# Four input-projection panels as seven block products, with x kept in DRAM during token mixing

## What is computed

```python
u = rmsnorm(x, ng[1]) * (1.0 + sc2) + sh2
proj = u @ P['w_in'][l]                       # 1024 -> 2816 columns
p_conv, p_rwkv, p_pool, p_sb = jnp.split(proj, IN_SPLITS, axis=-1)
# A short gated conv, B RWKV-7, C causal pooling, D stick-breaking attention -> y_a .. y_d
for i, y_i in enumerate((y_a, y_b, y_c, y_d)):
    merged = merged + jax.nn.sigmoid(u @ P['w_gate'][l, i]) * (y_i @ P['w_branch'][l, i])
x = x + g2 * (merged @ P['w_out'][l])
```

## Time and profile before

| | before |
|---|---|
| median of 3 runs | 3027.72 us (3027.41 to 3027.86) |
| profiled execution | 3027.79 us |
| its span | 3026.1 us |
| PE busy | 2991.8 us (99%) |
| DVE busy | 1426.4 us (47%) |
| ACT busy | 411.8 us (14%) |
| POOL busy | 1472.0 us (49%) |
| chain that ended last | PE 92%, POOL 4%, DVE 3%, issue 1% |

### The profile page before, as it was taken

The page is one execution under the profiler, slowest core; times in us unless marked ns, Lnnn a source line. Parts: engine busy times, 40 slices in busy tenths (PEclk is TensorE's granted clock), DMA queues, the critical chain, the costliest instruction groups (busy, mean ns, idle before and its releaser), DMA issues.

```text
span 3026.1 us, 48463 instructions
## 1 busy us (share of the span) xinstructions
PE 2991.8 (99%) x19566; PEld 2460.4 (81%) x19566; DVE 1426.4 (47%) x3125; ACT 411.8 (14%) x782; POOL 1472.0 (49%) x1527
## 2 busy tenths in 40 slices
PE   8999999999999999999999999999999999999999
PEld 5889888677777878898878898876777778789987
DVE  4446522464444464565244564324444444555642
ACT  2000002212111120000010000032021111200000
POOL 4879530212220348895468894312212213599943
PEclk9999999999999999999999999999999999999999
DMA  6543223541111424322245322334411114222221
GB/s 256 201 189 117 98 100 130 172 140 42 54 57 58 144 90 158 109 84 91 88 163 230 127 84 87 136 115 151 129 59 54 54 70 151 70 84 84 84 87 68
DMA packets 73535, 337.81 MB, mean 112 GB/s; under 512 B 10592, under 2 KB 27744, under 8 KB 40288
## 3 DMA queue, kind: packets, MB, share of 16 engines
q1 hardware_dynamic: 63936, 312.03, 28.5%
q0 software_dynamic: 6816, 18.88, 2.1%
q10 hardware_dynamic: 2560, 3.80, 0.4%
HBM read 326.55 MB, written 6.02 MB: 110 GB/s over the span
## 4 chain that ended last, share of the span: by engine, by line
PE 92%; POOL 4%; DVE 3%; issue 1%; DMA 0%; ACT 0%; SPq 0%; POOLq 0%; DVEq 0%
PE ps L1003 91%; DVE ws L2295 1%; DVE u L2295 1%; POOL masked_room L901 0%; DVE y L2295 0%; DMA ws<-w_ada 0%; POOL ws L860 0%; POOL ws L863 0%; ACT ws L1974 0%; POOL ws L864 0%; POOL ring L914 0%; POOL ws L868 0%; POOL ws L866 0%; POOL ws L849 0%; PE ps L1793 0%
## 5 line engine op out<-in xcount | busy, mean ns | idle before, releaser
L2295 DVE TENSOR_TENSOR ws<-ws,ps 128x272 f32<-128x272 f32 (+4 forms) x1650 | 620.2, 400 | 1110.1 <-PE ps L1003 1085.7
L1003 PE MATMUL ps<-u,ring 128*128 128x272 f32 (+1 forms) x4448 | 1035.7, 383 | 6.2 <-ACT u L1974 1.7
L1003 PEld LDWEIGHTS ps<-u,ring 128*128 128x128 f32 x4448 | 799.3, 190 | 181.5 <-issue 21.4
L1003 PE MATMUL ps<-y,ws 128*128 128x272 f32 (+1 forms) x1616 | 343.3, 348 | 0.0
L1003 PEld LDWEIGHTS ps<-y,ws 128*128 128x128 f32 x1616 | 265.4, 190 | 36.5 <-issue 4.5
L1974 ACT ACTIVATE ws<-ws 128x272 f32<-128x272 f32 (+5 forms) x226 | 137.0, 623 | 1105.5 <-DVE ws L2295 1054.0
L1003 PE MATMUL ps<-y,ring 128*128 128x272 f32 (+1 forms) x1376 | 277.0, 341 | 2.8 <-POOL ws L868 2.8
L1003 PEld LDWEIGHTS ps<-y,ring 128*128 128x128 f32 x1376 | 219.0, 190 | 33.1 <-POOL ws L868 3.8
L846 POOL TENSOR_TENSOR masked_room<-ring 128x512 f32<-128x512 f32 (+1 forms) x36 | 46.8, 1299 | 401.9 <-PE ps L1003 170.7
L1974 ACT ACTIVATE ws<-ps 128x272 f32<-128x272 f32 (+1 forms) x270 | 102.7, 395 | 864.3 <-PE ps L1003 864.2
L1003 PE MATMUL ps<-proj,ring 128*128 128x272 f32 x832 | 200.3, 393 | 1.5 <-DVE proj L2295 1.5
(11 more groups left out here) (248 smaller groups left out, 3825.0 us busy)
## 6 DMA issues: line engine op xcount, KB each, us to landing
ring<-w_up SPq DMA_DIRECT2D x88, 1024.0 KB, 4.9
proj<-w_ada SPq DMA_DIRECT2D x45, 1024.0 KB, 7.6
ring<-w_down SPq DMA_DIRECT2D x32, 1024.0 KB, 4.8
ring<-w_gate SPq DMA_DIRECT2D x32, 1024.0 KB, 4.9
ws<-w_ada SPq DMA_DIRECT2D x26, 1024.0 KB, 5.0
ring<-w_in SPq DMA_DIRECT2D x22, 1024.0 KB, 4.9
ws<-cache SPq DMA_DIRECT2D x128, 128.0 KB, 3.2
ws<-cache POOLq DMA_DIRECT2D x128, 128.0 KB, 3.4
```

Of the source, the lines that this page charges most:

```text
L1003: return nc.tensor.matmul(out, lhsT, rhs, start=start, stop=stop, skip_group_check=skip)
L2295: return V.tensor_tensor(out, a, b, op)
```

## The change

Panels 7 to 10 of the input projection are made by seven products of four matmuls (`split_in`) in place of four halves of eight. POOL makes the weight sums for each panel, three ahead and one when a12 has been used, S3 and S4 in the panel's own room in the ring; S1 and S2 have new rooms `in_s1` and `in_s2` in `ws`, of which the first covers the end of attention's `sa`, so panel 7's first sum waits for attention's last product. POOL's cache loads for the last three rounds stand between the sums. ACT copies out two results per panel and DVE makes the other additions (`in_sum`) at places in pooling, convolution and between token shifts. The banks are 1, 2, 3 and 4, 5, 7 in turn; the transposition of `own1` goes to bank 6.

The token sums T1 to T4 are made once by POOL, early, right after u is complete (`mix_token_sums`), for these panels and for the gates. They lie in x's room (`mix_tok`): SP stores x to DRAM (`x_kept`) as soon as it is complete, and loads it back behind the last gate panel (gate 23); DVE waits for it before it adds the output projection. Semaphores, the helpers `in_blocks`, `in_products`, `in_weights`, `in_act`, `in_dve` (waits on counts) and `in_out` (the result's place in `proj`) and the changed `split_tok` are left out below, as are blank lines.

```diff
+IN_SPLIT = (7, 8, 9, 10)
+IN_BANKS = {7: (1, 2, 3), 8: (4, 5, 7), 9: (1, 2, 3), 10: (4, 5, 7)}
+IN_ACT = {"first": 1, "c11": 2}
+IN_DVE = {"U2": 1, "U3": 2, "c22": 3, "c21": 4}
...
-        newT, at1 = carve(at1, P)
+        newT = sa[:, 896:1024]
+        in_s1, at1 = carve(at1 - 256, 4, P)
+        in_s2, at1 = carve(at1, 4, P)
...
+        mix_tok = x[:, :, :].rearrange("p a (b n) -> p (a b) n", n=HALF).rearrange("p (s k) n -> p s k n", s=4)
...
+        in_first, in_second, in_third = last_inner[:, :], masked_room[:, 544:544 + HALF], rtail[:, 512:512 + HALF]
...
+                            sp_.dma_start(x_kept, x[:, :, :]).then_inc(x_saved.sem, 16)
...
+                        if stage == "gate" and i == 23:
+                            sp_.dma_start(x[:, :, :], x_kept).then_inc(x_back.sem, 16)
...
+                def mix_token_sums():
                     b11, b12, b21, b22 = u[:, 0:4, 0:HALF], u[:, 0:4, HALF:T], u[:, 4:8, 0:HALF], u[:, 4:8, HALF:T]
-                    pool.wait_ge(pool_pe.sem, pool_pe.upto(l, 1))
-                    nc.gpsimd.tensor_tensor(split_t12[:, 0], b12, b11, ALU.subtract).then_inc(sp_sums.sem, 1)
+                    pool.wait_ge(x_saved.sem, x_saved.upto(l, 1))
+                    pool.wait_ge(up_done.sem, up_done.upto(l, U0[1] + 16))
+                    pool.wait_ge(us_done.sem, us_done.upto(l, 2))
+                    nc.gpsimd.tensor_tensor(mix_tok[:, 0], b12, b11, ALU.subtract).then_inc(sp_sums.sem, 1)
                     pool.wait_ge(sp_sums.sem, sp_sums.upto(l, 1))
-                    nc.gpsimd.tensor_tensor(split_t12[:, 1], b22, split_t12[:, 0], ALU.subtract).then_inc(sp_sums.sem, 1)
+                    nc.gpsimd.tensor_tensor(mix_tok[:, 1], b22, mix_tok[:, 0], ALU.subtract).then_inc(sp_sums.sem, 1)
                     pool.wait_ge(sp_sums.sem, sp_sums.upto(l, 2))
-                    nc.gpsimd.tensor_tensor(split_t4a, b21[:, 0:3], split_t12[:, 1, 0:3], ALU.subtract).then_inc(sp_sums.sem, 1)
-                    nc.gpsimd.tensor_tensor(split_t4b, b21[:, 3], split_t12[:, 1, 3], ALU.subtract).then_inc(sp_sums.sem, 1)
-                    pool.wait_ge(rp_pe.sem, rp_pe.upto(l, 2))
-                    pool.wait_ge(rp_dve.sem, rp_dve.upto(l, 1))
-                    nc.gpsimd.tensor_tensor(split_t3, b22, b12, ALU.subtract).then_inc(sp_sums.sem, 1)
+                    nc.gpsimd.tensor_tensor(mix_tok[:, 3], b21, mix_tok[:, 1], ALU.subtract).then_inc(sp_sums.sem, 1)
+                    nc.gpsimd.tensor_tensor(mix_tok[:, 2], b22, b12, ALU.subtract).then_inc(sp_sums.sem, 1)
+                def in_weight_sums(j):
+                    panel_wait(pool, l, "in", j)
+                    a11, a12, a21, a22 = in_blocks(l, j)
+                    if j == IN_SPLIT[0]:
+                        pool.wait_ge(at_pe.sem, at_pe.upto(l, 12))
+                    else:
+                        in_products(pool, l, j - 1, 5)
+                    nc.gpsimd.tensor_tensor(in_s1, a21, a22, ALU.add).then_inc(is_weights.sem, 1)
+                    in_weights(pool, l, j, 1)
+                    nc.gpsimd.tensor_tensor(in_s2, in_s1, a11, ALU.subtract).then_inc(is_weights.sem, 1)
+                    nc.gpsimd.tensor_tensor(a21, a11, a21, ALU.subtract).then_inc(is_weights.sem, 1)
+                def in_last_weight_sum(j):
+                    a11, a12, a21, a22 = in_blocks(l, j)
+                    in_products(pool, l, j, 3)
+                    in_weights(pool, l, j, 2)
+                    nc.gpsimd.tensor_tensor(a12, a12, in_s2, ALU.subtract).then_inc(is_weights.sem, 1)
...
+                mix_token_sums()
                 cache_loads(0, 4)
                 for to, at, ready in ((k_turned, P_K, kn_ready), (q_turned, P_Q, qp_done)):
                     pool.wait_ge(ready.sem, ready.upto(l, 1))
                     for a in (0, HD):
                         pool.dma_start(to[a:a + HD, :, :], proj[HD - a:P - a, at:at + 2, 0:TP])\
                             .then_inc(qk_turned.sem, 16)
-                cache_loads(4, 32)
-                split_token_sums()
+                cache_loads(4, 20)
+                for j in IN_SPLIT:
+                    in_weight_sums(j)
+                    if j < IN_SPLIT[-1]:
+                        cache_loads(4 * j - 8, 4 * j - 4)
+                    in_last_weight_sum(j)
...
+                def split_in(j, a, b):
+                    A, B, C = IN_BANKS[j]
+                    a11, a12, a21, a22 = in_blocks(l, j)
+                    def product(bank, w, v, start, frees=False):
+                        for k in range(4):
+                            m = mm(ps[:, bank, 0:HALF], w[:, k, :], v(k), start=start and k == 0, stop=k == 3, skip=True)
+                            if frees and k == 0:
+                                m.then_inc(part.sem, 1)
+                        return m
+                    def tok(k0, n0):
+                        return lambda k: u[:, k0 + k, n0:n0 + HALF]
+                    def sums(i):
+                        return lambda k: mix_tok[:, i, k, :]
+                    for n in range(a, b):
+                        if n == 0:
+                            panel(l, "in", j)
+                            pe_.wait_ge(in_done.sem, in_done.upto(l, 4 * j - 4))
+                            product(A, a11, tok(0, 0), True).then_inc(is_pe.sem, 1)
+                        elif n == 1:
+                            in_weights(pe_, l, j, 2)
+                            pe_.wait_ge(sp_sums.sem, sp_sums.upto(l, 2))
+                            product(B, in_s2, sums(1), True, True).then_inc(is_pe.sem, 1)
+                        elif n == 2:
+                            in_act(pe_, l, j, "first")
+                            product(A, a12, tok(4, 0), False).then_inc(is_pe.sem, 1)
+                        elif n == 3:
+                            in_weights(pe_, l, j, 3)
+                            pe_.wait_ge(sp_sums.sem, sp_sums.upto(l, 4))
+                            in_dve(pe_, l, j, "U2")
+                            product(B, a21, sums(2), False, True).then_inc(is_pe.sem, 1)
+                        elif n == 4:
+                            if j == IN_SPLIT[0]:
+                                pe_.wait_ge(at_act.sem, at_act.upto(l, 12))
+                            product(C, in_s1, sums(0), True).then_inc(is_pe.sem, 1)
+                        elif n == 5:
+                            in_dve(pe_, l, j, "U3")
+                            product(B, a22, sums(3), False, True).then_inc(is_pe.sem, 1)
+                        else:
+                            in_weights(pe_, l, j, 4)
+                            in_dve(pe_, l, j, "c22")
+                            product(C, a12, tok(4, HALF), False).then_inc(part.sem, 1)
...
-                        halves_in(28 + 4 * turn, 32 + 4 * turn)
-                halves_in(40, 42)
+                        split_in(7 + turn, 0, 7)
+                split_in(10, 0, 4)
                 pe_.wait_ge(se_dve.sem, se_dve.upto(l, 5))
-                nc.tensor.transpose(ps[:, 7, 0:P], own1, cmat(IDENT)).then_inc(se_pe.sem, 1)
+                nc.tensor.transpose(ps[:, 6, 0:P], own1, cmat(IDENT)).then_inc(se_pe.sem, 1)
                 pe_.wait_ge(pool_in.sem, pool_in.upto(l, 1))
                 pe_.wait_ge(at_act.sem, at_act.upto(l, 12))
+                pe_.wait_ge(in_done.sem, in_done.upto(l, 40))
                 for ft in range(2):
                     m = tile(ft, lp[:, PBD:PBD + 256], ft * P, pd, ft, 1)
                 m.then_inc(pool_pe.sem, 1)
-                halves_in(42, 44)
+                split_in(10, 4, 7)
...
+                for j in IN_SPLIT:
+                    in_products(act, l, j, 1)
+                    if j > IN_SPLIT[0]:
+                        in_dve(act, l, j - 1, "c21")
+                    f(in_first, ps[:, IN_BANKS[j][0], 0:HALF], ACT.Copy).then_inc(is_act.sem, 1)
+                    in_products(act, l, j, 3)
+                    f(in_out(j, 0, 0), ps[:, IN_BANKS[j][0], 0:HALF], ACT.Copy).then_inc(is_act.sem, 1)
...
+                if d == 1:
+                    dve.wait_ge(x_back.sem, x_back.upto(l, 1))
...
+                in_sum(l, 7, "U2")
-                evict(l, 28, 29)
-                evict(l, 29, 30)
+                in_sum(l, 7, "U3")
+                    if (ft, po) == (1, 0):
+                        in_sum(l, 7, "c22")
+                in_sum(l, 7, "c21")
-                evict(l, 30, 31)
+                in_sum(l, 7, "c12")
-                evict(l, 31, 32)
-                    evict(l, 32 + tap, 33 + tap)
+                    if tap == 0:
+                        in_sum(l, 8, "U2")
+                    if tap == 2:
+                        in_sum(l, 8, "U3")
-                evict(l, 35, 36)
+                in_sum(l, 8, "c22")
...
+            def in_sum(l, j, name):
+                A, B, C = IN_BANKS[j]
+                if name == "U2":
+                    if j > IN_SPLIT[0]:
+                        dve.wait_ge(in_done.sem, in_done.upto(l, 4 * j))
```

(58 more changed lines are left out.)

13 lines of the change are left out of this document (1 added, 12 removed).

## The result

| | before | after |
|---|---|---|
| median (10 runs each, same chip) | 3027.76 us (3027.36 to 3028.82) | 3033.64 us (3030.56 to 3038.51) |
| profiled execution, its span | 3027.79, 3026.1 us | 3033.25, 3031.6 us |
| PE busy | 2991.8 us | 2985.0 us |
| DVE busy | 1426.4 us | 1449.6 us |
| POOL busy | 1472.0 us | 1518.9 us |

The ratio is 1.002, with a 95% interval of 1.0011 to 1.0028: 5.9 us slower, about at the 6.06 us that I had set as the bound of no change. The forecast of 3013.9 us missed by 19.7 us, and the range did not hold the time. The matmuls did go: the count of PE's records falls by 64, that is 32 matmuls. Yet PE's busy time falls by only 6.8 us instead of 14.7, and runs differ by 8 us where they differed by 1.5.

A forecast was written before the change was run, and what follows sets the result against it. TensorE was taken to bound the touched stretch. 3027.79 - 14.67 us for removed matmuls gave 3013.1, plus 2 x 0.4 for stalls gave 3013.9 us; range 3012.5 to 3019.5 us.

The forecast's parts named there:

- the bound of no change: Whole kernel: a time within 0.2%, 6.06 us, counts as no change; that outcome was given 0.05.
- Matmuls removed: Input projection, panels 7 to 10: 32 fewer matmuls at 0.4586 us save 14.67 us, 14.9 as upper bound.
- Token sums early, x stored and loaded: POOL's early sums and x's trip to DRAM stay hidden: nothing, 0 to 1 us if bounded; store 13 to 25 us.
- POOL's rounds: Weight sums, page reads and cache loads per panel: 15.3 us if reads wait, 12.8 if beside sums, against PE's 14.7.
- Rival 1: POOL comes last: cache loads and panel 9's fourth sum 2 to 3 us late a layer; 3018.1 us, chance 0.29.
- DVE's sums: Five additions per panel for four evictions, 0.43 us each: taken as 0, at most 1 us a layer.
- The layout by hand from 628: DVE's sums placed against PE's needs from 628.02: all early, panel 7's c22 tightest with 0.5 us.
- The contention paragraph: POOL's sums overlapping DVE's work in the panels: each held by the other's operation, 1 to 2.5 us on POOL's round.
- The stretch that I looked at: Last part of the input projection: PE busy 67.09 of 67.60 us, so PE time saved is saved from the whole.
- Rival 3: Slower by DVE's order: 12 sums a layer before products, break-even at 0.61 us each, 3051 or 3061 us; chance 0.04.
- DVE late: PE waits for DVE before products 3, 5 or 6: Sign of late DVE in the panels, with DVE operations of 544 columns or more growing from 0.74 to over 1 us.
- the 0.4 us a layer: Allowance for stalls from POOL's rounds and DVE's sums together, added to the clean sum of 3013.1 us.

The follow-up runs named there:

- experiment 1: Changed kernel with POOL's four weight sums for each of panels 7 to 10 cut from 512 to 8 columns; 3013.13 us.
- experiment 2: Kernel before, input projection unchanged, with only the store and reload of x and the early token sums added; 3027.71 us.
- experiment 3: Changed kernel with POOL's first sums for panel 7 waiting until DVE has finished the sample attention's exponents; 3024.72 us.
- experiments 6 and 7: First: changed kernel, weight sums for panels 8 to 10 cut to 8 columns, 3021.89 us. Second: kernel before plus three unused POOL additions a layer, 3033.47 us.
- experiment 5: Changed kernel with POOL's weight sums for panel 7 alone cut to 8 columns, the others full; 3015.09 us.
- experiment 13: Changed kernel with panel 7's first sums waiting for the sample's exponents and six DVE additions moved, panel 9's U2 between token shifts; 3013.93 us.
- the memsets: Kernel before plus five POOL memsets of 128x512, released by attention's last product, writing SBUF and reading nothing; 3028.42 us.

## Why the prediction was wrong

- **Matmuls removed**: right. 14.67 us from the earlier trace rows gave 3013.1, and experiment 1 measured 3013.13; PE runs at 1.83 us a product here as in the gates. The lower end of the range, 3012.5, does not follow from the 14.9 us given for it (3027.79 - 14.9 = 3012.9); nothing hung on it.
- **Token sums early, x stored and loaded**: right. POOL issues its first cache loads 17.3 us later (492.30, 475.02 in the earlier trace rows), but PE's cache scores (538.89 in the profile after, 538.64 in the earlier trace rows) stay where they were within 0.25 us, and experiment 2 finds 0. The store lands in 8.3 us where I had estimated 13 to 25; nothing hung on it.
- **POOL's rounds**: right in outcome. Rival 1 did not come: no wait of PE for a cache load or a weight sum appears. The reads of page numbers, which the traces don't show, seem to run beside the sums: the loads of one round follow a last sum (666.43 to 667.74) at 669.32, and the first loads follow the last token sum (489.46 to 491.96) at 492.30, where I had counted 5.4 us for the reads and the first issue. That fits the case for which I had worked out 12.8 us a round.
- **DVE's sums, "I take 0, with an upper bound of 1 us a layer"**: the step that failed first. The layout by hand from 628 gave c22 0.5 us in hand, from durations of DVE without POOL. The contention paragraph had the right mechanism and the right row (1.06 us for 0.74), but charged it to POOL's round alone. Charged to DVE, four held operations ahead of c22 (0.78, 1.07, 1.07 and 1.07 us) come to 4.0 us, against 0.5 in hand, 3.5 us late: the measured wait is 3.3 us.
- **The stretch that I looked at**: the step that failed second. I opened it at 628.02, with panel 7's first product. The first three sums, however, are released by attention's last product at about 618.9, and from 612.5 to 621.6 the chain of the kernel before runs through DVE and not PE. The view of the chain that I read begins at 480 us, but I used only its piece from 625.16 on the earlier trace rows. That place costs 8.9 us by experiment 3 and was in no rival.
- **The clock**: in no sum. In the profile after, both gaps of 3.3 us in layer 0 were followed by matmuls at half pace: 1.36 and 1.74 us of the 9.5. It raised the loss by half. How often it falls differs from execution to execution (experiments 6 and 7), so no single figure for it would have been right for all.
- **Rival 3, slower by DVE's order**, was the right family with the wrong arithmetic. It spread the loss over twelve additions of at least 0.61 us each and so looked improbable. In fact one addition was late in each layer, by five times that, and a chain outside the twelve by 2.9 us.

In the list of what would show each step, "DVE late: PE waits for DVE before products 3, 5 or 6" came true at product 6; but the sign given beside it, operations of 544 columns growing to over 1 us, pointed at the wrong ones. The short ones grew most in proportion, from 0.18 to 1.24 us. The meeting of DVE and POOL, with the clock behind it, is the whole error: with one wait on POOL and DVE's order mended the kernel takes 3013.93 us. That this is the forecast's 3013.9 to the digit is luck: the 0.4 us a layer in it stood for other waits, and DVE's order is another one.

## What to carry to other kernels

Before work is given to an idle GpSimd, list the DVE operations with two SBUF inputs that can overlap it, from the moment that releases it and not from the stage that it serves, and add one whole GpSimd instruction for each that lies ahead of something TensorE waits for; short operations in a dependent chain pay most in proportion. Then compare the sum with what each addition has in hand, place by place, and add a term for the clock as a range from nothing to what the slow matmuls cost: behind gaps of 2.4 to 3.35 us it fell in some executions here and not in others. Where GpSimd's sums can't be moved, DVE's order can: put what PE waits for ahead of the held work, and after each move read which addition comes last now.

## What the runs showed of the hardware

- An addition of 32 columns takes 0.18 us alone and 1.24 to 1.28 us beside a GpSimd sum of 1.26 us; a GpSimd sum begun beside a DVE scan of 2.28 us takes 2.33. In these rows the engines alternate by whole instructions. GpSimd memsets slow neither (1.23 us for the addition of 1024 columns, 0.18 us for that of 32).
- A DVE addition with one input in a bank keeps its time beside a GpSimd sum: 0.44 us in experiment 5 (639.72, POOL's sum from 639.74), 0.43 us in the changed kernel (663.04, POOL's sum from 662.26 to 664.25).
- After the first PE gap of 3.35 us the granted clock was 0.74 over the next 6.5 us in both layers of the changed kernel's profile, and 1.00 in both layers of experiment 6's, behind the same gap; after gaps of 2.4 us it was 0.79 in one layer and 1.00 in the other. Eight matmuls in the gap kept it at 1.00 and gave back 3.25 us of the changed kernel's time.
- Kernels with such gaps scatter: 8.0 us between the extremes of ten runs in the changed kernel, 7.4 us in nine with the three sums alone and 6.0 us in ten of experiment 6, against 1.5 us in ten before and 0.6 us in four of experiment 13. The spread is no sure sign: the memsets, without such a gap, gave 2.7 us.
